# Merge, out-projection and query weights as slots of 512 columns by four channel blocks, in a two-layer hybrid backbone

## The chip, the cores and the metric

One Trainium2 chip, one core. The metric is the device time of one execution in microseconds (us), of which three were measured for the kernel before; their median counts.

## The reference, cut to what matters

Two layers run over 256 context tokens and 512 latent tokens, all of width 1024 and in float32. The weights that the change touches are those of the end of each layer's mixer, and of the query projection of the expert layer behind it:

```python
def merge(ys, gates_pre, w_branch, w_out):
    gates = jnp.split(gates_pre, N_BRANCH, axis=-1)
    acc = jax.nn.sigmoid(gates[0]) * (ys[0] @ w_branch[0])
    for i in range(1, N_BRANCH):
        acc = acc + jax.nn.sigmoid(gates[i]) * (ys[i] @ w_branch[i])
    return acc @ w_out
```

`gates_pre` are 4096 columns of the input projection `h @ w_in` (1024 by 10000), each `w_branch[i]` is 512 by 1024, `w_out` 1024 by 1024, and the query projection `peer_wq` 1024 by 2048. Behind it each token picks 128 of 16384 experts, whose rows of 1024 floats are gathered from `peer_u` (a dot product with the token) and `peer_v` (a weighted sum).

## The kernel before, in words

**Passes and tails.** Four passes run in turn: c0 and l0 (context and latent tokens of layer 0), then c1 and l1. Each ends in tails, one for each 256 tokens: c0 has one, l0 and l1 have two, c1 none. A tail is `merge` (all 16 pairs of a 256-column group j and a branch i), `outp` (out-projection, residual, second norm, transposes) and `query` (the query projection and the key scores). `merge` is written in `merge_part`, on the tensor, vector and scalar engines alike.

**Gathers beside it.** The expert layer (`peer`) is a second thread in the same programs. GpSimd issues one gather (128 rows of 4 KB) for each of the 128 slots of a token block (L3090), VectorE makes the dot product of it (L2252), TensorE sums the v rows (L1312). `side_by_side` puts so many steps of it between the pieces of a tail, by cost. Beside the second tail of l0 (stage t0) and of l1 (t1) run the 128 u gathers of the next block and their dots; beside the first tail of l0 runs the end of the expert layer of c0, with v sums on TensorE. c0's tail has the loading of later modulation weights beside it, and l1's first tail nothing: no gathers run then.

**Weight slots.** All weights go through a ring of `RING = 4` slots of 1 MB (`WRr`), in the order of `PLAN`, issued by SyncE (L3120) each as soon as the slot four places before it is marked `used`. A slot holds 256 columns by all 8 blocks of 128 input channels, so each partition gets 8 runs of 1 KB; a branch's weights (4 blocks) fill half a slot. `merge_part` on TensorE takes a gate slot and a branch slot together at the start of a unit and frees both at its end:

```python
wg = weight(("gate", pn, f, j, i_))
wb = weight(("branch", pn, f, j, i_), BB)
...
if m == 1:
    used(("gate", pn, f, j, i_))
    used(("branch", pn, f, j, i_))
```

**Results.** Each result of 128 channels by 256 tokens takes half of a PSUM bank. A gate bank is read by ScalarE (L2810, tanh into `GS`, three buffers of 256), a branch bank by VectorE (L2017 or L2020, the sum by L2022), an out-projection bank by L2048 and L2051, a query bank by L2858 or L2173. `bank` hands the banks out in turn: five where the expert layer runs beside (`BANKS`), else all eight; it waits until the last user of the bank has been read.

**Woven attention.** In c0 and in l1's first tail the merge of branches 0 to 2 is woven between the steps of the windowed attention (`attn_mix`), which in l1 takes seven banks per step from the same ring. In l0's first tail it is woven with the convolution (`conv_late`).

## Time and profile before

| what | value |
|---|---|
| runs (us) | 6261.03, 6256.57, 6257.69 |
| median | 6257.69 us |
| span of the profiled execution | 6280.9 us |
| TensorE busy | 4128.8 us (66%) |
| VectorE busy | 3226.1 us (51%) |
| GpSimd busy | 2794.8 us (44%) |
| ScalarE busy | 711.8 us (11%) |
| DMA moved | 1739.24 MB, mean 277 GB/s |
| gathers' queue q0 | 380032 packets, 1384.49 MB, 59.9% of 16 engines' span |
| SyncE's queue q1 | 314896 packets, 304.03 MB, 15.4% |

The page gives the profiled execution by its span from the first to the last instruction, and no other time of it; that span is 23.2 us (0.4%) above the median of the timed runs. Shares are averages over stages with different limits. By their instructions the five tails lie at about 364 to 685 us (c0), 1565 to 1983 (l0, first), 1983 to 2330 (l0, second, stage t0), 4197 to 4587 (l1, first) and 4587 to 4930 (l1, second, stage t1).

### The profile page before, as it was taken

Reading aid. Unit: us, or ns where it says so; the run is one execution under the profiler, and the core shown is the slowest. Engines: PE = TensorE matmul, PEld = TensorE weight load, DVE = VectorE, ACT = ScalarE, POOL = GpSimd, SP = SyncE. Lnnn points to the kernel's source line nnn. Section 1 sums busy time; section 2 is a strip of 40 time slices with the busy share of each in tenths; the row PEclk is TensorE's granted clock in tenths of the full one; section 3 lists DMA queues with packets and bytes.
Section 4 is the critical chain, followed back from the end, with each engine's and each line's share of the span. In section 5 each row is a group of like instructions: output and inputs, shape, how many; then the busy total and the mean of one; then the engine's idle time right before and its main releaser. Section 6 shows DMA issues by size and latency. Waiting matters only on the chain.

```text
span 6280.9 us, 65214 instructions
## 1 busy us (share of the span) xinstructions
PE 4128.8 (66%) x23760; PEld 2525.3 (40%) x23760; DVE 3226.1 (51%) x7726; ACT 711.8 (11%) x1572; POOL 2794.8 (44%) x2606
## 2 busy tenths in 40 slices
PE   5899767777988864544443668888977533333346
PEld 4677544335666652221110235557766300000012
DVE  3422788565625856556444216443277564654430
ACT  1221112123010011000000001233100000000000
POOL 0000243555322446767767630000034677777765
PEclk8999887889998986665555789999988755555557
DMA  6645565988886999999999971112579999999998
GB/s 221 219 156 166 190 208 199 316 312 291 290 302 231 323 340 343 355 352 360 361 367 361 368 262 43 57 43 80 171 257 326 348 353 361 369 358 365 359 367 328
DMA packets 721231, 1739.24 MB, mean 277 GB/s; under 512 B 88912, under 2 KB 371408, under 8 KB 719248
## 3 DMA queue, kind: packets, MB, share of 16 engines
q0 software_dynamic: 380032, 1384.49, 59.9%
q1 hardware_dynamic: 314896, 304.03, 15.4%
q10 hardware_dynamic: 25984, 46.56, 2.1%
q8 instruction: 189, 3.10, 0.2%
q14 instruction: 130, 1.06, 0.0%
HBM read 1706.98 MB, written 27.89 MB: 276 GB/s over the span
## 4 chain that ended last, share of the span: by engine, by line
PE 31%; issue 21%; DMA 10%; POOL 10%; DVE 9%; another core or an unknown queue 2%; ACT 2%; SPq 0%; POOLq 0%; ACTq 0%; DVEq 0%
POOL arena L3090 10%; PE bank L1219 7%; PE bank L1312 6%; DMA arena<-in_peer_v,arena 5%; PE bank L794 4%; PE bank L1273 3%; PE bank L1225 3%; DMA arena<-in_peer_u,arena 3%; DVE arena L2252 2%; PE bank L805 1%; PE bank L876 1%; PE bank L1174 1%; DMA arena<-in_w_in 1%; PE bank L1253 1%
## 5 line engine op out<-in xcount | busy, mean ns | idle before, releaser
L3090 POOL DMA_INDIRECT arena<-in_peer_u,arena x1280 | 1413.4, 1104 | 2173.6 <-DVE arena L2162 951.5
L1312 PE MATMUL bank<-arena 128*32 128x256 f32 x10240 | 1216.4, 541 | 1451.7 <-DMA arena<-in_peer_v,arena 1175.5
L2252 DVE CUSTOM_DVE_ANT_0 arena<-arena 128x1024 f32<-128x1024 f32 x1280 | 1540.5, 1223 | 1013.7 <-DMA arena<-in_peer_u,arena 922.4
L3090 POOL DMA_INDIRECT arena<-in_peer_v,arena x1280 | 1354.6, 1058 | 880.6 <-PE bank L1312 357.6
L1312 PEld LDWEIGHTS bank<-arena 128*32 128x32 f32 x10240 | 311.2, 130 | 2306.7 <-DMA arena<-in_peer_v,arena 1705.3
L1219 PE MATMUL bank<-arena 128*128 128x256 f32 x2560 | 618.3, 397 | 90.7 <-issue 55.8
L794 PE MATMUL bank<-arena 128*128 128x512 f32 (+1 forms) x1600 | 636.9, 552 | 30.2 <-issue 26.6
L1219 PEld LDWEIGHTS bank<-arena 128*128 128x128 f32 x2560 | 504.8, 200 | 187.1 <-issue 108.7
L794 PEld LDWEIGHTS bank<-arena 128*128 128x128 f32 x1600 | 320.4, 207 | 299.5 <-issue 279.4
L1225 PE MATMUL bank<-arena 128*128 128x256 f32 x1280 | 306.5, 382 | 2.3 <-ACT arena L2810 2.3
L1273 PE MATMUL bank<-arena 128*128 128x256 f32 x1280 | 292.6, 390 | 23.2 <-issue 23.2
L1273 PEld LDWEIGHTS bank<-arena 128*128 128x128 f32 x1280 | 248.2, 196 | 65.6 <-issue 31.0
L1225 PEld LDWEIGHTS bank<-arena 128*128 128x128 f32 x1280 | 239.1, 190 | 47.4 <-ACT arena L2810 13.2
L764 PE MATMUL bank<-arena 128*128 128x128 f32 x408 | 91.9, 351 | 243.9 <-DVE arena L1477 139.4
L2020 DVE SCALAR_TENSOR_TENSOR arena<-arena,bank 128x256 f32<-128x256 f32 x120 | 50.3, 420 | 340.4 <-PE bank L1225 294.3
L2893 ACT ACTIVATE arena<-arena 128x16 f32<-128x16 f32 x80 | 17.2, 216 | 1784.6 <-DVE arena L2252 1085.1
L1562 DVE SCALAR_TENSOR_TENSOR arena<-arena 128x512 f32<-128x512 f32 (+1 forms) x360 | 213.8, 658 | 5.8 <-DVE arena L1562 0.4
L805 PE MATMUL bank<-arena 128*128 128x256 f32 (+1 forms) x960 | 213.5, 382 | 2.7 <-ACT arena L2596 2.2
L805 PEld LDWEIGHTS bank<-arena 128*128 128x128 f32 x960 | 179.5, 205 | 40.1 <-issue 17.6
L764 PEld LDWEIGHTS bank<-arena 128*128 128x128 f32 x408 | 62.0, 179 | 286.3 <-issue 175.9
L1253 PE MATMUL bank<-arena 128*128 128x256 f32 x640 | 148.9, 395 | 25.7 <-issue 19.4
L3052 POOL DMA_DIRECT2D arena<-in_mod_w x20 | 15.1, 756 | 321.0 <-PE bank L832 321.0
(271 smaller groups left out, 3905.3 us busy)
## 6 DMA issues: line engine op xcount, KB each, us to landing
arena<-in_w_in SPq DMA_DIRECT2D x152, 1024.0 KB
arena<-in_mod_w POOLq DMA_DIRECT2D x20, 2048.0 KB, 11.6
arena<-in_peer_wq SPq DMA_DIRECT2D x40, 1024.0 KB
arena<-in_w_branch SPq DMA_DIRECT2D x60, 512.0 KB
arena<-in_w_out SPq DMA_DIRECT2D x20, 1024.0 KB
arena<-in_peer_u,arena POOLq DMA_INDIRECT x1280
arena<-in_peer_v,arena POOLq DMA_INDIRECT x1280
arena<-in_w_branch SPq DMA_DIRECT2D x40, 256.0 KB
```

What stands on the lines that cost most here:

```text
L764: return nc.tensor.transpose(dst, src, eye)
L794: i = mm(b[:, 0:p.n], w[:, k, m * P:(m + 1) * P], HTk(p)[:, k, :], start=(k == 0), stop=(k == KD - 1))
L805: i = mm(b[:, 0:n], HTk(p)[:, k, t * P:(t + 1) * P], w[:, k, c0:c0 + n], start=(k == 0), stop=(k == KD - 1))
L876: i = mm(b[:, 0:hi - lo], w[:, k, m * P:(m + 1) * P], HTk(p)[:, k, lo:hi], start=(k == 0), stop=(k == KD - 1))
L1219: i = mm(b[:, 0:W], wg[:, k, m * P:(m + 1) * P], HTk(p)[:, k, half], start=(k == 0), stop=(k == KD - 1))
L1225: i = mm(b[:, 0:W], wb[:, k, m * P:(m + 1) * P], YS(p, i_)[:, k, half], start=(k == 0), stop=(k == BB - 1))
L1253: i = mm(b[:, 0:W], ACC[:, k, x % 2 * P:(x % 2 + 1) * P], w[:, k, :], start=(k == 0), stop=(k == KD - 1))
L1273: i = mm(b[:, 0:W], w[:, k, m * P:(m + 1) * P], H2T[:, k, :], start=(k == 0), stop=(k == KD - 1))
L1312: i = mm(banks[6 + g // 2][32 * j:32 * j + 32, (g % 2) * W:(g % 2 + 1) * W], G["ws"][:, g, 32 * m:32 * m + 32], G["row"][ROW_BUFFER["v", i ...
L1562: v.scalar_tensor_tensor(y[:, m, :], cp[:, m, j:j + p.n], tap, y[:, m, :], ALU.mult, ALU.add)\
L2252: v.tensor_tensor_reduce(u, u, G["h2"][it % 2], 1.0, 0.0, ALU.mult, ALU.add, G["dots"][:, n:n + 1]).then_inc(*pr.step("dot", it, n))
L3090: fl.done(eng.indirect_dma_start(G["row"][x], None, table, bass.IndirectOffsetOnAxis(ids[:, n:n + 1], 0)), f"row_landed{x}", (kind + "_lan ...
```

## The change

For the tails' weights a slot becomes 512 columns by four channel blocks: runs of 2 KB, the same 1 MB, and a branch's weights now fill a slot. Gate, out-projection and query groups take two slots each (`e` = 0, 1), whose partial sums meet in the same bank; each slot is awaited where it is first used and freed after its own use. The 16 merge units of a tail become 8 units of three slots, with the same matmuls in another order. Two results of 256 share a bank, so ScalarE and VectorE read 512 columns at a time (two `GS` buffers of 512 in place of three of 256). The out-projection's matmuls have 512 moving columns in place of 256, so there are half as many. Costs that place the side thread are 3.6 for each of the six pieces of a unit. In woven tails attention and merge no longer share a ring: attention has five banks in l1 (four in c0), the merge three, the modulation one (`BESIDE`), and c0's main ring has seven.

```diff
+WIDE = 2 * W
+QK = KD // 2
...
+BESIDE = {"attn": (0, 1, 2, 5, 7), "attn_c": (0, 1, 2, 5), "merge": (3, 4, 6), "mod": (7,)}
...
-    every = [(j, i) for j in range(D // W) for i in range(4)]
+    every = [(j, i) for j in range(D // WIDE) for i in range(4)]
...
-        GS, PRD = H2[:, 0, 0:3 * W].rearrange("p (b t) -> p b t", b=3), H2[:, 0, 3 * W:4 * W]
+        GS = rows4(H2[:, 0, :], 2)
...
+        def wide(src):
+            return [(lambda w: w.rearrange("p (k n) -> p k n", k=QK), src)]
+        def plan_wide(name, a, c0):
+            for e in range(2):
+                plan(name + (e,), wide(w_view(a, KD)[:, e * QK:(e + 1) * QK, c0:c0 + WIDE]))
+        def plan_gate(l, pn, f, j, i):
+            plan_wide(("gate", pn, f, j, i), w_in[l], C_GATE + i * D + j * WIDE)
+        def plan_branch(l, pn, f, j, i):
+            plan(("branch", pn, f, j, i), branch_rows(l, i, j))
...
-                for j in range(D // W):
-                    plan(("out", pn, f, j), whole(w_view(ins["w_out"][l], KD)[:, :, j * W:(j + 1) * W]))
-                for j in range(HEADS * 256 // W):
-                    plan(("wq", pn, f, j), whole(w_view(ins["peer_wq"][l], KD)[:, :, j * W:(j + 1) * W]))
+                        plan_gate(l, pn, f, j, i)
+                        plan_branch(l, pn, f, j, i)
+                for j in range(D // WIDE):
+                    plan_wide(("out", pn, f, j), ins["w_out"][l], j * WIDE)
+                for g in range(HEADS // 2):
+                    plan_wide(("wq", pn, f, g), ins["peer_wq"][l], g * WIDE)
...
-            def bank(name):
-
-                x = taken["next"] % taken["banks"]
-                taken["next"] = x + 1
+            def bank(name, ring=None):
+                if ring is None:
+                    x = taken["next"] % taken["banks"]
+                    taken["next"] = x + 1
+                else:
+                    x = BESIDE[ring][taken[ring] % len(BESIDE[ring])]
+                    taken[ring] += 1
...
-                    ba = [bank(("as", pn, t, f, g)) for g in range(AKV)]
-                    bc = bank(("asc", pn, t, f)) if len(kb) > 4 else None
+                    ba = [bank(("as", pn, t, f, g), ring) for g in range(AKV)]
+                    bc = bank(("asc", pn, t, f), ring) if len(kb) > 4 else None
...
+                ring = "merge" if woven(p) and f == 0 and part[0][1] == 0 else None
                 for j, i_ in part:
-                    wg = weight(("gate", pn, f, j, i_))
-                    wb = weight(("branch", pn, f, j, i_), BB)
-                    for m in range(2):
-                        b = bank(("gate", pn, f, j, i_, m))
-                        for k in range(KD):
-                            i = mm(b[:, 0:W], wg[:, k, m * P:(m + 1) * P], HTk(p)[:, k, half], start=(k == 0),
-                                   stop=(k == KD - 1))
-                        i.then_inc(*mn.step("full", ("gate", pn, f, j, i_, m)))
-                        yield 3.4
-                        b = bank(("branch", pn, f, j, i_, m))
-                        for k in range(BB):
-                            i = mm(b[:, 0:W], wb[:, k, m * P:(m + 1) * P], YS(p, i_)[:, k, half], start=(k == 0),
-                                   stop=(k == BB - 1))
-                        i.then_inc(*mn.step("full", ("branch", pn, f, j, i_, m)))
-                        if m == 1:
-                            used(("gate", pn, f, j, i_))
-                            used(("branch", pn, f, j, i_))
-                        yield 1.8
+                    b = {}
+                    for e in range(2):
+                        name = ("gate", pn, f, j, i_, e)
+                        w = weight_wide(name)
+                        for q in range(2):
+                            if e == 0:
+                                b[q] = bank(("gate", pn, f, j, i_, "pair", q), ring)
+                            for m in range(2):
+                                for k in range(QK):
+                                    i = mm(b[q][:, m * W:(m + 1) * W], w[:, k, (2 * q + m) * P:(2 * q + m + 1) * P],
+                                           HTk(p)[:, e * QK + k, half], start=(e == m == k == 0), stop=(e == m == 1 and k == QK - 1))
+                            if e:
+                                i.then_inc(*mn.step("full", ("gate", pn, f, j, i_, "pair", q)))
+                            elif q:
+                                i.then_inc(*mn.step())
+                            if q:
+                                used(name)
+                            yield 3.6
+                    name = ("branch", pn, f, j, i_)
+                    w = weight_wide(name)
+                    for q in range(2):
+                        b = bank(("branch", pn, f, j, i_, q), ring)
+                        for m in range(2):
+                            for k in range(BB):
+                                i = mm(b[:, m * W:(m + 1) * W], w[:, k, (2 * q + m) * P:(2 * q + m + 1) * P], YS(p, i_)[:, k, half],
+                                       start=(k == 0), stop=(k == BB - 1))
+                        i.then_inc(*mn.step("full", ("branch", pn, f, j, i_, q)))
+                        if q:
+                            used(name)
+                        yield 3.6
...
-                    for j in range(D // W):
-                        w = weight(("out", pn, f, j))
+                    for j in range(D // WIDE):
                         b = bank(("out", pn, j, t))
-                        for k in range(KD):
-                            i = mm(b[:, 0:W], ACC[:, k, x % 2 * P:(x % 2 + 1) * P], w[:, k, :], start=(k == 0), stop=(k == KD - 1))
-                        i.then_inc(*mn.step("full", ("out", pn, j, t)))
-                        if x % 2:
-                            used(("out", pn, f, j))
-                        yield 3.5
+                        for e in range(2):
+                            w = weight_wide(("out", pn, f, j, e))
+                            for k in range(QK):
+                                i = mm(b[:, :], ACC[:, e * QK + k, x % 2 * P:(x % 2 + 1) * P], w[:, k, :],
+                                       start=(e == 0 and k == 0), stop=(e == 1 and k == QK - 1))
+                            if e:
+                                i.then_inc(*mn.step("full", ("out", pn, j, t)))
+                            elif x % 2:
+                                i.then_inc(*mn.step())
+                            if x % 2:
+                                used(("out", pn, f, j, e))
+                            yield 3.5
...
+                    if what == "quad":
+                        g, (e, q) = n[0], divmod(n[1], 2)
+                        name = ("wq", pn, f, g, e)
+                        w = weight_wide(name)
+                        if e == 0:
+                            open_[q] = bank(("wq", pn, f, "pair", 2 * g + q))
+                        for m in range(2):
+                            for k in range(QK):
+                                i = mm(open_[q][:, m * W:(m + 1) * W], w[:, k, (2 * q + m) * P:(2 * q + m + 1) * P],
+                                       H2T[:, e * QK + k, :], start=(e == m == k == 0), stop=(e == m == 1 and k == QK - 1))
+                        if e:
+                            i.then_inc(*mn.step("full", ("wq", pn, f, "pair", 2 * g + q)))
+                        elif q:
+                            i.then_inc(*mn.step())
+                        if q:
+                            used(name)
...
+            share_banks(len(banks) - 1)
...
+                    for _ in range(4):
                         yield 0
...
+                    for q in range(2):
+                        eng.wait_ge(*at("gsig", pn, f, j, i_, q))
+                        eng.wait_ge(*at("full", ("branch", pn, f, j, i_, q)))
+                        b = bank_of(("branch", pn, f, j, i_, q))
+                        acc, g = query_pair(2 * j + q), GS[:, q, :]
                         if i_ == first_branch(p, f):
...
+                            v.scalar_tensor_tensor(acc, g, 1.0, b[:, :], ALU.add, ALU.mult).then_inc(*mn.step("read", ("branch", pn, f, j, i_, q)))
                         else:
+                            v.scalar_tensor_tensor(g, g, 1.0, b[:, :], ALU.add, ALU.mult).then_inc(*mn.step("read", ("branch", pn, f, j, i_, q)))
                             eng.wait_ge(*mn.latest())
...
+                            v.tensor_tensor(acc, acc, g, ALU.add).then_inc(*mn.step())
+                        fl.mark(("gs_free", pn, f, j, i_, q), mn.sem)
...
+                past = None
                 for j, i_ in part:
...
+                    yield 0
+                    yield 0
+                    for q in range(2):
+                        if past is not None:
+                            eng.wait_ge(*at("gs_free", pn, f, *past, q))
+                        eng.wait_ge(*at("full", ("gate", pn, f, j, i_, "pair", q)))
+                        b = bank_of(("gate", pn, f, j, i_, "pair", q))
+                        act(GS[:, q, :], b[:, :], ACT.Tanh, scale=0.5).then_inc(*mn.step("gsig", pn, f, j, i_, q))
+                        fl.mark(("read", ("gate", pn, f, j, i_, "pair", q)), mn.sem)
                         yield 0
...
+                    past = (j, i_)
```

TensorE in the merge of stage t0. Names: L1219 is the gate matmul, L1225 the branch matmul before; `weights_loaded0` to `3` are the landings of the four slots, `l0_scalar` and `l0_vector` reads by the other engines. Before, one unit of 1.5 MB (256 columns of one branch):

```order
L1219 MATMUL bank2<-arena 128x256 [waits l0_scalar,weights_loaded3,weights_loaded2]
L1219 MATMUL bank2<-arena 128x256 x7
L1225 MATMUL bank3<-arena 128x256 [waits l0_scalar]
L1225 MATMUL bank3<-arena 128x256 x3
L1219 MATMUL bank4<-arena 128x256 [waits l0_vector]
L1219 MATMUL bank4<-arena 128x256 x7
L1225 MATMUL bank0<-arena 128x256 [waits l0_scalar]
L1225 MATMUL bank0<-arena 128x256 x3
```

and now one unit of 3 MB (512 columns), with L1255 for gates and L1270 for branches:

```order
L1255 MATMUL bank2<-arena 128x256 [waits l0_scalar,weights_loaded3]
L1255 MATMUL bank2<-arena 128x256 x7
L1255 MATMUL bank3<-arena 128x256 [waits l0_scalar]
L1255 MATMUL bank3<-arena 128x256 x7
L1255 MATMUL bank2<-arena 128x256 [waits weights_loaded0]
L1255 MATMUL bank2<-arena 128x256 x7
L1255 MATMUL bank3<-arena 128x256 x8
L1270 MATMUL bank4<-arena 128x256 [waits l0_scalar,weights_loaded1]
L1270 MATMUL bank4<-arena 128x256 x7
L1270 MATMUL bank0<-arena 128x256 [waits l0_vector]
L1270 MATMUL bank0<-arena 128x256 x7
```

Before, one instruction waits for two slots every 24 matmuls; now each slot is awaited alone, with 16 matmuls on each, and between the last matmul into a bank and the first of its next use lie 32 to 48 other matmuls in place of 24.

TensorE in the first tail of l1, where an attention step (from L1140) follows a merge piece. Before:

```order
L1219 MATMUL bank4<-arena 128x256 [waits l1_vector,weights_loaded1,weights_loaded0]
L1219 MATMUL bank4<-arena 128x256 x7
L1140 MATMUL bank7<-arena 128x128 [waits l1_scalar,l1_vector]
L1144 MATMUL bank5<-arena 128x256
L1144 MATMUL bank6<-arena 128x256
L1146 MATMUL bank5<-arena 128x128
L1146 MATMUL bank6<-arena 128x128
L1150 MATMUL bank5<-arena 128x128
L1150 MATMUL bank6<-arena 128x128
L1155 MATMUL bank7<-arena 128x128 [waits l1_tensor]
```

and now (the step begins at L1171):

```order
L1255 MATMUL bank6<-arena 128x256 [waits weights_loaded1]
L1255 MATMUL bank6<-arena 128x256 x7
L1255 MATMUL bank3<-arena 128x256 x8
L1171 MATMUL bank0<-arena 128x128 [waits l1_scalar,l1_vector]
L1175 MATMUL bank5<-arena 128x256
L1175 MATMUL bank7<-arena 128x256
L1177 MATMUL bank5<-arena 128x128
L1177 MATMUL bank7<-arena 128x128
L1181 MATMUL bank5<-arena 128x128
L1181 MATMUL bank7<-arena 128x128
L1186 MATMUL bank0<-arena 128x128 [waits l1_tensor]
```

The bank of the first score (`asc`), taken by the step's first instruction, is now `bank0`, which the copy of the first transposed probabilities of the previous step (ScalarE L2755 before) has to have read; before it was the bank of eight allocations ago.

## Rows read from the trace of the kernel before

**Rows 1.** The page, 40 slices of 157 us: DMA in tenths, rate.

```profile
DMA  6645565988886999999999971112579999999998
GB/s 221 219 156 166 190 208 199 316 312 291 290 302 231 323 340 343 355 352 360 361 367 361 368 262 43 57 43 80 171 257 326 348 353 361 369 358 365 359 367 328
```

**Rows 2.** Busy us of each engine by stretch, clock, DMA share, rate.

```profile
1565.00:1827.00 262.00, 261.33 (x1537) 170.52 (x1537) 122.88 (x201) 23.47 (x48) 91.08 (x91) 1.00 0.88 290
...
2011.00:2207.00 196.00, 159.54 (x669) 134.75 (x667) 159.95 (x428) 12.68 (x33) 98.93 (x82) 0.90 0.96 335
2207.00:2262.00 55.00, 33.61 (x145) 28.88 (x145) 40.82 (x76) 5.29 (x10) 21.24 (x18) 0.81 0.93 329
2262.00:2330.00 68.00, 64.17 (x321) 56.93 (x321) 42.71 (x81) 12.37 (x22) 31.84 (x27) 0.98 0.99 360
2011.00:2330.00 319.00, 257.32 (x1134) 220.55 (x1132) 243.48 (x584) 30.33 (x65) 152.01 (x126) 0.90 0.96 339
...
4612.00:4930.00 318.00, 257.10 (x1134) 220.39 (x1133) 240.78 (x578) 30.60 (x65) 152.05 (x127) 0.90 0.95 331
```

**Rows 3.** Waits of 2011 to 2207 us: total, times, longest.

```profile
PE bank L1219 <- issue: 28.3, 8, 7.8
...
DVE arena L2252 <- DMA arena<-in_peer_u,arena: 10.2, 3, 8.1
...
PE bank L1219 <- DMA arena<-in_w_branch: 7.5, 1, 7.5
```

**Rows 4.** Timeline, SyncE queue and TensorE, 2071 to 2092 us: start, us.

```profile
2071.22 0.37 SPq L3120 DMA_DIRECT2D arena<-in_w_in  x1
2071.64 2.29 SPq L3120 DMA_DIRECT2D arena<-in_w_branch  x2
2083.63 0.37 SPq L3120 DMA_DIRECT2D arena<-in_w_in  x1
...
2091.43 2.04 PE L1219 MATMUL bank<-arena 128*128 128x256 f32 x4 [7.84 <-issue]
```

**Rows 5.** DMA queues, 2011 to 2330 us: packets, MB, share of 16 engines.

```profile
q0 software_dynamic: 18432, 67.12, 57.2%
q1 hardware_dynamic: 36068, 36.95, 35.5%
```

**Rows 6.** The same, 4612 to 4930 us.

```profile
q1 hardware_dynamic: 33216, 34.08, 33.1%
```

**Rows 7.** The same, 4197 to 4466 us, with no gathers.

```profile
q1 hardware_dynamic: 24096, 24.12, 29.8%
```

**Rows 8.** The same, 5000 to 6200 us, gathers almost alone.

```profile
q0 software_dynamic: 117423, 427.54, 95.0%
```

**Rows 9.** Chain that ended last, 1820 to 1985 us: start, us.

```profile
1838.04 16.56 DMA arena<-in_norm_g
```

**Rows 10.** Timeline, 1845 to 1880 us, first out-projection of l0.

```profile
1856.66 6.40 PE L1253 MATMUL bank<-arena 128*128 128x256 f32 x16 [6.30 <-DVE arena L2048]
...
1877.73 0.86 PEld L764 LDWEIGHTS bank<-arena 128*128 128x128 f32 x8 [4.13 <-DVE arena L2062]
```

**Rows 11.** Groups of instructions by line: busy, mean ns, idle before.

```profile
L1219 PE MATMUL bank<-arena 128*128 128x256 f32 x2560 | 618.3, 397 | 90.7 <-issue 55.8 <-DMA arena<-in_w_branch 16.6 <-DVE arena L2111 7.1
...
L2810 ACT ACTIVATE arena<-bank 128x256 f32<-128x256 f32 x160 | 61.1, 382 | 773.1 <-PE bank L1219 698.4 <-issue 25.2 <-DVE arena L2158 22.9
...
L2020 DVE SCALAR_TENSOR_TENSOR arena<-arena,bank 128x256 f32<-128x256 f32 x120 | 50.3, 420 | 340.4 <-PE bank L1225 294.3 <-issue 26.7 <-ACT arena L2760 15.9
...
L2755 ACT ACTIVATE arena<-bank 128x512 f32<-128x512 f32 x64 | 34.8, 589 | 4.6 <-PE bank L1174 3.3 <-remote 1.3
...
L1422 DVE TENSOR_TENSOR arena<-bank,arena 128x512 f32<-128x512 f32 x26 | 18.0, 691 | 0.9
```

**Rows 12.** Waits of 4197 to 4466 us, second layer, first half.

```profile
PE bank L1174 <- ACT arena L2772: 21.3, 16, 2.3
...
PE bank L1225 <- ACT arena L2810: 2.3, 5, 0.5
```

134 lines of the change are left out of this document (57 added, 77 removed).

## The prediction

> **What bounds the kernel now.** I read the page's slices first: between about 2000 and 3600 us, and again from about 4600 us to the end, the DMA row stands at 8 or 9 tenths and the rate near 340 to 370 GB/s [rows 1]. Those are the stretches with expert gathers. The tails that the change touches lie partly inside them, so I asked for busy times by stretch next. In stage t0 (second tail of l0) the DMA share is 0.96 from the first gather at 2011 us to the end at 2330 us, while TensorE is busy 257.3 of 319 us and VectorE 243.5. In t1 it is 0.95 of 318 us, TensorE 257.1 [rows 2]. So both stages are bound by the DMA engines, not by an engine that computes. In l0's first tail it is the other way: TensorE is busy 261.3 of 262 us in the merge, at DMA share 0.88 [rows 2].
>
> The waits say how TensorE feels the full DMA. In the merge of t0 it lost 28.3 us "issue" in 8 waits and 7.5 us to a branch weight [rows 3]; "issue" is idle time for which the profile shows no releaser, and the timeline tells what it is: SyncE issued a gate and a branch slot at 2071.22 and 2071.64, the unit before ended when the next two slots were issued, at 2083.63, and TensorE went on only at 2091.43 [rows 4]. These waits are late weights. VectorE on the other side waited only 10.2 us for u rows [rows 3]: the gathers are ahead, the weights behind.
>
> **The change, part by part.** All against a span of 6280.9 us, which is 23.2 us above the median of the runs; the terms are taken off the median, since 0.4% of any of them is nothing.
>
> *Runs of 2 KB.* The bytes stay, the number of runs halves. Price of a run of 1 KB inside t0: q1 took 35.5% of 319 us, 113 us, for 36.95 MB, so 16 x 113 us / 36.95 MB, 50 ns per run. A gather row of 4 KB there took 57.2% of 319 us x 16 / 67.12 MB, 178 ns [rows 5]. A straight line through both has a fixed part of 7.5 ns per run, so runs of 2 KB save 3.7 of 50 ns, 7.5%, which is 8.4 us of t0. The other end comes from stretches where each queue is nearly alone: 54.5 ns per KB without gathers (24.12 MB in 29.8% of 269 us) and 175 ns per row of the gathers (427.54 MB in 95.0% of 1200 us) [rows 7, 8]. That gives a fixed part of 14.4 ns and a saving of 13%, 15 us. I take 11 us, between them, since the two pairs of rows are about equally near; in t1, with q1 at 33.1% of 318 us [rows 6], 10 us. As the stages are bound by this, the saving is on the path: 21 us, with ends 16 and 28.
>
> The Trainium skill ("DMA: Bandwidth & Descriptors", Why small descriptors are slow) gives each packet about 3 cycles on top of one per 32 bytes: 35 for 1 KB against 67 for 2 KB, an estimate of 4% or 9 us for both stages, by which the time would be 12 us higher than my forecast. No row here counts cycles.
>
> *Slots freed one by one, all four full.* Now at most two slots are asked for when a unit ends; after the change each slot has three others' work, 48 matmuls, to land in, against 24. It fills the idle DMA time, at most 4% of 319 us (13 us) in t0 and 5% of 318 us (16 us) in t1 [rows 2]. Some of it stays: barriers between stages (t0's out-projection has TensorE busy for 33.6 of 55 us, at DMA share 0.93 [rows 2]), and the time in which VectorE's dots hold the gathers. I take a third, 9 us for both; ends 0 and 29.
>
> *Out-projection.* Half as many matmuls, twice as wide: the same columns, so TensorE's time stays. In l0's first tail the chain waits 16.56 us for the row of the second norm [rows 9], and VectorE reads no out-projection bank before it, so TensorE runs out of its five banks and stands 6.30 us [rows 10]. Now four results need four banks, so it does not stand; and one slot rather than two is ahead of the norm rows in the queue when the merge ends. 1 MB costs 3.3 us alone (24.12 MB in 80 us [rows 7]) and 8.6 us beside gathers (36.95 MB in 319 us [rows 5]). What comes behind, a wait of 4.13 us of the last transposes for VectorE [rows 10], is late next. I take 4 us; ends 0 and 9. c0 and l1 have no gathers beside their out-projection and gain nothing.
>
> *Reads of 512.* An instruction of 256 columns takes 382 ns on ScalarE and 420 ns on VectorE, one of 512 takes 589 and 691 ns [rows 11]: less in all, but VectorE is not the bound. At a stage's end the last result waits for two of 691 in place of two of 420 ns, 0.54 us more. At three such ends each in c0 and l1's first tail nothing covers that: 3.3 us lost. The gates' longer hold and the two `GS` buffers cost nothing, since ScalarE waits for TensorE there (698.4 us of waits before L2810 [rows 11]); were that cover gone, it would be 0.2 us a read.
>
> *Bank rings in the woven tails.* In l1 the first instruction of an attention step now waits for ScalarE's copy of the first transposed probabilities. Where a gate has just ended (every third step, 5 of them) ScalarE does a tanh of 512 and then that copy, 589 ns each [rows 11]: 1.2 us x 5, 6 us lost. Against that, 2.3 us of waits of branch matmuls for gate reads go [rows 12]. Ends: 0 and 12 us. In c0 a step takes four banks from a ring of four, read a whole step before, so nothing. The modulation's own bank is read at once after its group; nothing.
>
> Sum: -21 - 9 - 4 + 3 + 4 = -27 us, and 6257.7 - 27 = 6231 us.
>
> **Rivals.** *A, the weights catch up altogether.* Here two queues share an engine run by run. 1 KB of weights against a row of 4 KB then has 50 of 228 ns, 16 x 1024 B in 228 ns or 72 GB/s, and the late fetch of [rows 4], 1.57 MB in some 18 us (87 GB/s), is near it. With 2 KB it would be 93 of 271 ns, 121 GB/s: 25.2 MB of merge weights come in 208 us, and most idle DMA time goes. All high ends: -28 - 29 - 9 + 3 = -63, 6195 us. Against it: VectorE must find its dots' rows in what is left. The Trainium skill ("DMA: Bandwidth & Descriptors", Queues, rings and completion order) says that an engine drains a whole packet of some 9 to 17 descriptors before it turns to another queue, by which the length of a run need not change the share as the line through [rows 5] has it; no row here shows the turns.
>
> *B, the wait moves.* What the weights gain the gathers lose: VectorE, which hardly waits for rows now [rows 3], waits for them, the branch banks are read later, and only the cheaper runs at their low end remain, without the 4 us. -16 + 7 = -9, 6249 us. For it speaks the share of 0.96 [rows 2]: there is little left to hand over.
>
> *C, slower: the small rings.* If each attention step of l1 (16) and c0 (8) waits for ScalarE's or VectorE's read, as TensorE already does once per step (21.3 us in 16 waits, the longest 2.3 [rows 12]), by 2.3 us, that is 55 us against the 34 gained: 6279 us. It decides from 34 / 24 = 1.4 us a step. Against it: the order shows only every third step with a gate's tanh in the way.
>
> *D, the runs are not 2 KB.* Should the queue cut them to 1 KB again, the 21 us go: 6252 us.
>
> **How the numbers follow.** Forecast 0.50, A 0.20, B 0.17, C 0.10, D 0.03. The likeliest case gives 6231 us and by itself reaches from about 6215 to 6245. The range goes down to A and up to just short of C: 6194 to 6266 us. A measurement of this kernel can tell about 0.2%, 12.5 us, from no change. Faster by more: nearly all of the forecast, and A: 0.68. Within: B, D and the forecast's upper edge: 0.21. Slower: C and a little: 0.11.
>
> **What would show it.** Right: q1's packets fall by about 90,000 (five tails of 36,864 runs of 1 KB, halved) at the same MB; t0 and t1 are each some 15 us shorter at an unchanged DMA share near 0.96; the "issue" waits of the gate line there shrink below 15 us; the stand of 6.30 us is gone; l1's first tail is some 5 us longer. Wrong: t0 and t1 unchanged with VectorE's waits for u rows grown (B), or shorter by 28 us and more (A); attention steps in l1 and c0 with a wait before each first score (C); q1 with as many packets as before (D).

## The result, and the profile after

The changed kernel takes 6214.5 us (median of 4 runs, 6209.27 to 6220.0); the kernel before, run beside it, takes 6258.6 us (6256.57 to 6261.03). The ratio is 0.9929, with a 95% interval from 0.9915 to 0.9943: 44 us faster. The forecast was 6231 us with 6194 to 6266 as its range; what was measured lies about half way between it and rival A's 6195 us.

The page of the kernel after, span 6212.5 us (the execution itself 6214.72 us); the second line shown is DMA in tenths over 40 slices:

```profile
PE 4094.5 (66%) x23440; PEld 2448.4 (39%) x23440; DVE 3201.4 (52%) x7526; ACT 693.6 (11%) x1470; POOL 2814.9 (45%) x2606
...
DMA  6555465898996989999999971122479999999999
...
q0 software_dynamic: 380032, 1384.49, 60.3%
q1 hardware_dynamic: 221936, 304.03, 15.0%
```

q1 carries the same 304.03 MB in 92,960 fewer packets, as announced, so rival D is out. Its share of the whole span hardly moved, and no share on the page tells where 44 us went. For that I measured each tail from TensorE's timeline, from its first gate matmul to the start of what follows it: the next layer or tail for the first tails, the first v sum for t0 and t1. c0's tail is taken to the start of its last query matmul:

| us | before | before, run again | after | after, run again |
|---|---|---|---|---|
| c0, tail | 305.2 | 305.4 | 306.2 | 308.1 |
| l0, first tail | 418.4 | 418.5 | 409.3 | 411.8 |
| l0, second tail (t0) | 389.5 | 388.9 | 371.2 | 371.6 |
| of it, merge to the first out-projection matmul | 231.3 | 230.2 | 212.0 | 212.4 |
| l1, first tail | 390.8 | 391.0 | 391.5 | 391.5 |
| l1, second tail (t1) | 358.6 | 351.9 | 338.8 | 336.6 |

The three tails beside gathers give 9 or 7, 17 to 18 and 13 to 22 us, together 43 on the mean. For t1 the spread is wide because the two executions of the kernel before differ by 6.7 us there. The rest of the program, mostly gathers alone, scatters by 10 us and more from one execution to the next (the last 1330 us took 1334.7 and 1325.6 before, 1317.9 and 1324.8 after), so I leave it out. In t0 the whole gain lies before the out-projection. Busy times there (columns as in [rows 2]: busy us of TensorE, its weight loads, VectorE, ScalarE and GpSimd, then clock, DMA share and GB/s; the second row is TensorE's idle piece at the merge's end):

```profile
2000.00:2152.00 152.00, 143.28 (x651) 123.66 (x649) 133.95 (x362) 9.36 (x18) 81.38 (x71) 0.99 1.03 381
2152.00:2184.00 32.00, 0.19 (x1) 0.22 (x2) 31.59 (x53) 0.60 (x1) 17.98 (x12) 0.53 0.96 344
2184.00:2232.00 48.00, 32.55 (x80) 15.20 (x80) 32.13 (x56) 5.28 (x10) 20.78 (x17) 0.82 0.80 290
2232.00:2301.00 69.00, 64.49 (x321) 57.17 (x321) 42.85 (x78) 11.68 (x18) 32.64 (x26) 0.97 0.97 349
2000.00:2301.00 301.00, 240.51 (x1052) 196.25 (x1050) 240.52 (x547) 26.92 (x47) 152.78 (x126) 0.91 0.97 355
```

In these first 152 us the DMA engines move 381 GB/s; in the 152 us from 2011 us of the kernel before they moved 333, and in its whole merge 335 [rows 2]. Then TensorE stands for 32 us in which VectorE is busy for 31.59. The waits in the merge of t0, of TensorE and of VectorE, to be held against [rows 3]:

```profile
PE bank L1298 <- DVE arena L2077: 32.0, 1, 32.0
PE bank L1255 <- DVE arena L2169: 4.9, 1, 4.9
...
PE bank L1270 <- DMA arena<-in_w_branch: 1.3, 1, 1.3
```

```profile
DVE arena L2310 <- DMA arena<-in_peer_u,arena: 13.0, 7, 8.1
```

Each line gives the total, how many waits, and the longest. The late weights are gone: 28.3 us of "issue" and 7.5 us for a branch weight have become 1.3 us. In their place stands one wait of 32.0 us: the first out-projection matmul (L1298) needs the last sum of the merge (L2077). The timelines of TensorE and of VectorE there:

```profile
2139.74 3.62 PE L1255 MATMUL bank<-arena 128*128 128x256 f32 x16
2144.68 7.17 PE L1270 MATMUL bank<-arena 128*128 128x256 f32 x32 [1.33 <-DMA arena<-in_w_branch]
2183.81 2.90 PE L1298 MATMUL bank<-arena 128*128 128x512 f32 x3 [31.95 <-DVE arena L2077]
```

```profile
2154.71 1.22 DVE L2310 CUSTOM_DVE_ANT_0 arena<-arena 128x1024 f32<-128x1024 f32 x1
...
2156.37 2.29 DVE L2188 TENSOR_TENSOR arena<-arena 128x2048 f32<-128x2048 f32 x1
2158.70 2.77 DVE L2194 TENSOR_TENSOR arena<-arena 128x256 f32<-128x256 f32 x8
2161.50 2.29 DVE L2196 TENSOR_REDUCE arena<-arena 128x128 f32<-128x2048 f32 x1
...
2182.30 0.69 DVE L2075 SCALAR_TENSOR_TENSOR arena<-arena,bank 128x512 f32<-128x512 f32 x1
2183.02 0.69 DVE L2077 TENSOR_TENSOR arena<-arena 128x512 f32<-128x512 f32 x1
```

TensorE has its last branch result ready near 2152 us. VectorE reads it at 2182.30, behind dots (L2310) and routing work (L2188 to L2196) that its order puts ahead, and it is never idle meanwhile. In t1 it is the same: TensorE's idle piece is 27.5 us, and VectorE is busy for 27.6 of the 28 us from 4736 us. So in the kernel after, VectorE ends the merges of t0 and t1.

What did it wait for before? The kernel before, VectorE in the merge of t0 (1983.3 to 2214.6 us):

```profile
DVE arena L2020 <- issue: 19.1, 4, 8.0
```

L2020 reads a branch result. Each of the four waits ended 0.1 us after TensorE's last matmul into that result (L1225), and each such result followed a wait of TensorE that [rows 3] counts as "issue": for those 19.1 us VectorE stood for results that TensorE could not yet make. They are as long as the whole difference: 231.3 - 19.1 = 212.2, against 212.0 us measured. That fit is in part luck, since two smaller changes cancel: VectorE's busy time fell from 191.4 to 188.7 us, and its waits for gathered rows grew from 10.2 to 13.0. The second execution of the kernel before, with a merge of 230.2 us, has 19.5 us of the same waits:

```profile
DVE arena L2020 <- issue: 11.1, 4, 4.8
...
DVE arena L2017 <- PE bank L1225: 8.4, 2, 4.4
```

That is the theory the experiments are to test: **late weights cost this stage only through VectorE's idle time; the DMA engines do not bound it.** Its rival is the sentence of the prediction, "both stages are bound by the DMA engines".

### The profile page after: what moved, and what is told of

The parts are those of the page before. It is cut to its first block and busy times, and to the rows that moved or that the text cites. A ratio compares the mean times of both kernels' runs of the same rounds, so it can differ in the third digit from the quotient of the medians.

```text
span 6212.5 us, 63979 instructions
## 1 busy us (share of the span) xinstructions
PE 4094.5 (66%) x23440; PEld 2448.4 (39%) x23440; DVE 3201.4 (52%) x7526; ACT 693.6 (11%) x1470; POOL 2814.9 (45%) x2606
## 3 DMA queue, kind: packets, MB, share of 16 engines
q1 hardware_dynamic: 221936, 304.03, 15.0%
q14 instruction: 126, 1.03, 0.0%
## 5 line engine op out<-in xcount | busy, mean ns | idle before, releaser
L1369 PE MATMUL bank<-arena 128*32 128x256 f32 x10240 | 1203.4, 538 | 1433.9 <-DMA arena<-in_peer_v,arena 1181.6
L2310 DVE CUSTOM_DVE_ANT_0 arena<-arena 128x1024 f32<-128x1024 f32 x1280 | 1540.5, 1223 | 1035.7 <-DMA arena<-in_peer_u,arena 911.2
L1255 PE MATMUL bank<-arena 128*128 128x256 f32 x2560 | 579.0, 385 | 25.1 <-DVE arena L2169 12.3
L1255 PEld LDWEIGHTS bank<-arena 128*128 128x128 f32 x2560 | 487.7, 193 | 109.5 <-issue 42.0
L1326 PE MATMUL bank<-arena 128*128 128x256 f32 x1280 | 293.5, 391 | 27.4 <-issue 27.4
L1270 PE MATMUL bank<-arena 128*128 128x256 f32 x1280 | 290.5, 384 | 8.6 <-DVE arena L2073 3.6
L1270 PEld LDWEIGHTS bank<-arena 128*128 128x128 f32 x1280 | 243.1, 192 | 50.4 <-issue 5.0
L785 PE MATMUL bank<-arena 128*128 128x128 f32 x408 | 93.0, 354 | 229.9 <-DVE arena L1534 129.5
L1298 PE MATMUL bank<-arena 128*128 128x512 f32 x320 | 145.2, 612 | 63.8 <-DVE arena L2077 32.0
L2075 DVE SCALAR_TENSOR_TENSOR arena<-arena,bank 128x512 f32<-128x512 f32 x60 | 41.2, 686 | 274.9 <-PE bank L1270 273.9
L785 PEld LDWEIGHTS bank<-arena 128*128 128x128 f32 x408 | 63.1, 181 | 271.8 <-issue 171.4
```

The lines of the kernel that those rows point to most:

```text
L785: return nc.tensor.transpose(dst, src, eye)
L1255: i = mm(b[q][:, m * W:(m + 1) * W], w[:, k, (2 * q + m) * P:(2 * q + m + 1) * P], HTk(p)[:, e * QK + k, half], start=(e == m == k == 0), ...
L1270: i = mm(b[:, m * W:(m + 1) * W], w[:, k, (2 * q + m) * P:(2 * q + m + 1) * P], YS(p, i_)[:, k, half], start=(k == 0), stop=(k == BB - 1))
L1298: i = mm(b[:, :], ACC[:, e * QK + k, x % 2 * P:(x % 2 + 1) * P], w[:, k, :], start=(e == 0 and k == 0), stop=(e == 1 and k == QK - 1))
L1326: i = mm(open_[q][:, m * W:(m + 1) * W], w[:, k, (2 * q + m) * P:(2 * q + m + 1) * P], H2T[:, e * QK + k, :], start=(e == m == k == 0), st ...
L1369: i = mm(banks[6 + g // 2][32 * j:32 * j + 32, (g % 2) * W:(g % 2 + 1) * W], G["ws"][:, g, 32 * m:32 * m + 32], G["row"][ROW_BUFFER["v", i ...
```

## The experiments

They ran in three groups, each beside the kernel before: 6253.5 us for e0 to e3, 6048.4 us for e4 to e7, 6262.2 us for e8 to e11. Why the second group is 3.3% shorter is taken up at the end; within a group the ratio counts, across groups the length of the tails, which did not change with it.

**e0, the kernel before again.**

> The kernel before, once more, with a profile: a control. Both theories: no difference from the runs of before. Its profile is to show how far the stretches of two executions of one program differ: the first profile of before was 22 us longer than the median of its runs, and the stretch of pure gathers at the end (L1312 from 4946 us on) was 17 us longer there than in the changed kernel. If that is scatter, this profile has that stretch within 5 us of the changed kernel's 1318 us.

It took 6251.9 us, ratio 0.9989 (0.9976 to 1.0003). This is what no change looks like. Its tails stand in the table above. Its stretch of pure gathers at the end took 1325.6 us, not within 5 us of the changed kernel's 1318 as expected, but 9 us shorter than in the first execution of the same program: scatter, and more of it than expected.

**e1, runs of 1 KB again.** Each slot of 512 columns comes as two transfers of 256 columns (four for the attention branch); slots, order and freeing stay as changed, in all five tails.

```diff
...
-            return [(lambda w: w.rearrange("p (k n) -> p k n", k=QK), src)]
+            return [((lambda w, h=h: w.rearrange("p (k n) -> p k n", k=QK)[:, :, h * W:(h + 1) * W]),
+                     src[:, :, h * W:(h + 1) * W]) for h in range(2)]
```

> The changed kernel with each wide slot loaded by two DMAs of 256 columns (four for the attention branch), so that the runs are 1 KB again; slots, banks and order stay. Theory 1 (cheaper runs carry most of the gain): 21 us slower than the changed kernel, 6235 us, with the DMA share of t0 unchanged and its length up by 10 us. Theory 2 (slots freed one by one, all four full, carry it): within 6 us of 6214.5 us. Theory 3 (share of an engine by run: with 1 KB the weights get 50 of 228 ns beside gathers): over 30 us slower, and the waits of the gate line for weights are back.

It took 6213.3 us, ratio 0.9928 (0.9912 to 0.9943), not to be told from the changed kernel's 0.9929: theory 2's forecast, and far from the other two. t0 took 371.0 us, merge to out-projection 211.9. The same stretch as the last row above, TensorE's waits and VectorE's in the merge, and q1 in the stretch:

```profile
2000.00:2301.00 301.00, 247.62 (x1049) 199.10 (x1047) 240.25 (x547) 27.14 (x47) 151.37 (x125) 0.93 1.00 355
```

```profile
PE bank L1257 <- DMA arena<-in_w_in: 11.5, 6, 5.3
PE bank L1272 <- DMA arena<-in_w_branch: 10.7, 5, 5.0
```

```profile
DVE arena L2077 <- PE bank L1272: 4.6, 2, 3.8
```

```profile
q1 hardware_dynamic: 35477, 36.00, 36.8%
```

The runs of 1 KB cost what they were said to cost: q1 took 0.368 x 301 / 36.00 = 3.08 us of all 16 engines per MB, against 0.327 x 301 / 35.56 = 2.77 us with runs of 2 KB (19696 packets of q1 in that stretch, 35.56 MB, 32.7%), 11% more. The weights were later by 21 us as well. Neither reached the end of t0, because TensorE had 32 us to spare. In t1, where it had 27.5, a little did: the merge to the out-projection took 210.8 us against 207.8 and 207.5 in the two executions of the changed kernel, with 7.0 us of VectorE's waits for late results, where the changed kernel has none:

```profile
DVE arena L2077 <- PE bank L1272: 7.0, 2, 5.2
```

From the changed kernel to e1 the DMA share of the stretch rose from 0.97 to 1.00 at the same 355 GB/s: a high share did not mean that the engines had nothing left to give.

**e2, slots freed together.** In the second tails the two gate slots are marked used only with the branch slot, at the unit's end.

```diff
-                            if q:
+                            if q and f == 0:
                                 used(name)
...
                         if q:
+                            if f:
+                                for e in range(2):
+                                    used(("gate", pn, f, j, i_, e))
                             used(name)
```

> The changed kernel, but in the second tails of l0 and l1 (t0 and t1) the three slots of a merge unit are freed together at its end, as before. Theory 1: the depth gave 9 us, so 6223 us, waits of the gate line for weights come back to some 15 us per tail. Theory 2: 30 us slower, 6245 us. Theory 3: under 5 us slower, since weights of 2 KB runs arrive fast enough.

It took 6206.7 us, ratio 0.9922 (0.9908 to 0.9936), the changed kernel's again; here theory 3's forecast came out, so no theory has both e1 and e2. t0 took 371.1 us, though TensorE waited:

```profile
PE bank L1255 <- DMA arena<-in_w_in: 15.9, 7, 3.7
PE bank L1301 <- issue: 10.3, 1, 10.3
PE bank L1270 <- DMA arena<-in_w_branch: 6.5, 4, 2.3
```

In t1 the merge to the out-projection took 211.1 us, 3 more than in the changed kernel, as in e1, and VectorE waited there:

```profile
DVE arena L2078 <- PE bank L1270: 5.3, 2, 3.9
```

**e3, both undone.**

> Both edits together. Theory 1: the two add up, 30 us slower than the changed kernel, 6245 us, so most of the 44 us is gone; what is left comes from out-projection and reads. Theory 2: as much slower as with the freeing alone. Theory 3: as much slower as with the short runs alone.

It took 6234.2 us, ratio 0.9966 (0.9954 to 0.9978): 21 us more than e1 and 28 more than e2. t0 took 383.6 us and t1 352.3. TensorE's waits in the merge of t0, then VectorE's:

```profile
PE bank L1257 <- DMA arena<-in_w_in: 17.8, 7, 4.4
PE bank L1272 <- DMA arena<-in_w_branch: 12.8, 2, 7.5
PE bank L1303 <- issue: 9.8, 1, 9.8
```

```profile
DVE arena L2080 <- PE bank L1272: 7.6, 3, 3.2
DVE arena L2080 <- issue: 4.3, 1, 4.3
DVE arena L2078 <- PE bank L1272: 3.6, 2, 3.2
```

With both undone VectorE stands 15.5 us for late results, and merge to out-projection is 223.9 us, 11.9 over the 212.0 of the changed kernel. With one undone it stood 4.6 us (e1) or not at all (e2) and there was no loss. In t1 each alone cost 3 us, and both together 13 (221.0 us, with 16.5 us of such waits). So the two remedies are not terms of a sum, and none of the three theories foretold that: either alone brings nearly all weights inside VectorE's time, and the second has little or nothing left to give.

**e4, narrow out-projection results.** Weights stay in wide slots; each result of 256 columns has its own bank, and VectorE reads 256 columns at a time.

```diff
-                        b = bank(("out", pn, j, t))
+                        b = [bank(("out", pn, j, h, t)) for h in range(2)]
...
-                                i = mm(b[:, :], ACC[:, e * QK + k, x % 2 * P:(x % 2 + 1) * P], w[:, k, :],
+                                    i = mm(b[h][:, 0:W], ACC[:, e * QK + k, x % 2 * P:(x % 2 + 1) * P],
+                                           w[:, k, h * W:(h + 1) * W],
...
```

> The changed kernel with the out-projection's results 256 columns wide again, one bank for each and VectorE reading 256 at a time; the weights stay in wide slots. Theory (the out-projection gained because TensorE hands over and VectorE reads half as many, twice as large results): the out stage of l0's first tail goes from 33.8 us back to about 43, the other out stages by 0 to 3, the kernel by +8 to +14 us, to about 6226. Rival (it gained because its weights, and the merge's ring of banks ahead of it, are no longer late): the out stage stays within 3 us and the kernel within 5 us of the changed one, 6209 to 6220.

It took 6006.2 us, ratio 0.9933 (0.9917 to 0.9949), not to be told from the changed kernel's 0.9929. So the rival's forecast came out and the theory's 8 to 14 us did not. l0's first tail took 412.2 us, hardly more than the changed kernel's 409.3 and 411.8 and far from the 418.5 of before; from its first out-projection matmul to its first query matmul it took 51.4 us, against 50.9 and 50.6 in the changed kernel and 59.5 and 59.0 before; the matmuls themselves span 37.5 us, against 34.4 and 44.0. But the row of the second norm landed earlier in this execution, which can hide a loss. VectorE's first work behind that row, in the changed kernel and in e4:

```profile
1848.32 1.23 DVE L2096 SCALAR_TENSOR_TENSOR arena<-arena 128x1024 f32<-128x1024 f32 x1 [23.05 <-DMA arena<-in_norm_g]
...
1868.16 0.69 DVE L2091 COPY arena<-bank 128x512 f32<-128x512 f32 x1 [0.91 <-PE bank L785]
```

```profile
1814.07 1.22 DVE L2100 SCALAR_TENSOR_TENSOR arena<-arena 128x1024 f32<-128x1024 f32 x1 [18.95 <-DMA arena<-in_norm_g]
...
1840.56 0.69 DVE L2095 COPY arena<-bank 128x512 f32<-128x512 f32 x1 [1.53 <-PE bank L785]
```

From the row to the last copy it is 20.5 us with wide results, 27.2 with narrow ones, 24.8 in the kernel before (1854.72 to 1879.56). VectorE's wait for the row was 26.91 us before, 23.05 after, 18.95 here. So of the 8.6 us from 59.5 to 50.9, 3.9 are the earlier row and 4.3 the shorter way from it to the last copy. The earlier row is not scatter: it landed 26.8 and 26.9 us after the first out-projection matmul in the two executions of before, and 22.6 to 22.9 in nine of the twelve with the change in them (18.9 to 21.4 in the other three, 18.9 being e4's). That the 4.3 us come from wide results is argued from the rows behind the norm, not shown by the time of e4.

**e5, dots spread.** The cost of a merge piece in the second tails is 2.8 in place of 3.6, so `side_by_side` puts less of the side thread between them: 70 dots in place of 78 in the merge of t0, and three blocks of routing work (L2188 to L2196) in place of four.

```diff
-                            yield 3.6
+                            yield 3.6 if f == 0 else 2.8
...
-                        yield 3.6
+                        yield 3.6 if f == 0 else 2.8
```

> The changed kernel with the cost of a unit of the second tails' merges set from 3.6 to 2.8, which moves some 8 of the 83 units of routing and dots out of each merge into the out-projection and the query (a dot keeps VectorE for 1.30 us, 1220 ns and 82 ns). Theory (the merge of t0 and t1 ends at VectorE since the weights are in time): merge and gap together fall from 212 us by about 10, out and query absorb the dots in VectorE's idle time (43 of 117 us there), so t0 and t1 are each 8 to 10 us shorter and the kernel takes about 6195 to 6199 us. Rival (the DMA engines bound the whole stage, share 0.97 between 2000 and 2301): what the merge gains, out and query give back; the kernel within 5 us of the changed one.

It took 5983.1 us, ratio 0.9896 (0.9878 to 0.9915): the lowest ratio of all kernels that compute the reference. t0 took 364.0 us and t1 331.7, each 7 us less than in the changed kernel (7.6 and 4.9 less than in its second execution), where the theory had 8 to 10. The merge of t0, and TensorE's wait at its end:

```profile
1946.70:2140.50 193.80, 172.81 (x770) 147.72 (x770) 171.54 (x422) 12.64 (x23) 92.16 (x77) 0.95 0.96 350
```

```profile
PE bank L1298 <- DVE arena L2077: 14.1, 1, 14.1
```

VectorE is busy 17.2 us less in the merge (188.7 before this edit), the merge is 18.2 us shorter, and 11.0 us of it come back behind. The dots now lie ahead of the norm, whose wait by TensorE (L785) grew to 19.0 us. No transfer was made smaller or dropped, only the order of VectorE's work was changed, with the gathers that follow it: that order bounds the merge.

**e6, more for VectorE.** One more instruction of 512 columns, without effect, behind each result of the second tails' merges.

```diff
+                        if f == 1:
+                            eng.wait_ge(*mn.latest())
+                            v.tensor_tensor(acc, acc, acc, ALU.max).then_inc(*mn.step())
```

> The changed kernel with one more VectorE instruction of 512 columns, of no effect, behind each result of the second tails' merges: 16 of 691 ns in each, 11.1 us. Theory (VectorE bounds these merges): t0 and t1 are each 9 to 11 us longer, the kernel takes 6233 to 6237 us. Rival (the DMA engines bound them; VectorE waits 13 us for gathered rows in the merge, and would spend the new work there): each at most 3 us longer, the kernel within 6 us of the changed one.

It took 6017.0 us, ratio 0.9945 (0.9928 to 0.9961). t0 took 380.1 us and t1 346.1, 8.9 and 7.3 us more than after, just under the 9 to 11 of the theory and far over the rival's 3. The new line in the merge of t0, and TensorE's wait:

```profile
L2080 DVE TENSOR_TENSOR arena<-arena 128x512 f32<-128x512 f32 x16 | 11.1, 691 | 0.5
```

```profile
PE bank L1298 <- DVE arena L2080: 34.0, 1, 34.0
```

Of 11.1 us of new work 8.6 show in the merge (220.6 us in place of 212.0). The rest went into VectorE's waits for gathered rows, 10.0 us in place of 13.0. The wait grew by 2 us only, since TensorE's matmuls were held up too (7.2 us for L2075 in place of 4.8).

**e7, half of each gate slot loaded.** In the second tails only two of the four channel blocks of each gate slot are loaded; the rest of the slot keeps what it held.

```diff
...
+            for e in range(2):
+                plan(("gate", pn, f, j, i, e), [((lambda w: w.rearrange("p (k n) -> p k n", k=QK)[:, 0:2]),
+                                                 w_view(w_in[l], KD)[:, e * QK:e * QK + 2, c0:c0 + WIDE])])
```

> The changed kernel with only half of each gate slot loaded in the second tails' merges (2 of 4 pieces of 128 input channels; the rest of the slot keeps what it held, so the gates of these halves are computed from wrong weights). 16 slots of 1.05 MB halved are 8.4 MB less in each of t0 and t1, at the 355 GB/s of 2000 to 2301 some 24 us of the DMA engines. Theory (VectorE bounds the merge once the weights are in time): merge and gap stay near 212 us, less what VectorE waited for gathered rows (13 us); the kernel is 0 to 15 us faster, 6200 to 6215. Rival (both stages are bound by the DMA engines): t0 and t1 each about 20 us shorter, the kernel near 6175.

It took 5989.4 us, ratio 0.9904 (0.9886 to 0.9922). 16.8 MB fewer were loaded; t0 took 364.3 us and t1 334.9, 7 and 4 us less, where a DMA-bound stage would have lost 20 to 24 each. So the bytes are not free, but they are worth between a sixth and a third of that. TensorE still stood 32.0 us for L2077's counterpart. VectorE's wait for gathered rows fell from 13.0 to 7.9 us, which is 5.1 of the 6.1 us by which the merge got shorter.

**e9, the changed kernel again, and e8, fewer bytes with the dots spread.** e8 joins the edits of e5 and e7, so it too leaves out half of each gate slot.

> The changed kernel itself, as the measure for the three beside it. Ratio to the kernel before as at first, 0.993; t0 371 us, t1 338 us.

> Cost 2.8 for the second tails' merge units (dots spread, as in e5_dots_spread) and only half of each of their gate slots loaded (as in e7_gate_half_loaded; the gates of the other halves are computed from wrong weights). Theory (the DMA engines are not what ends t0 and t1, even with the dots spread): the fewer bytes give what they gave alone, 4 to 7 us in each; t0 about 358 us, t1 about 327 us. Rival (once VectorE is relieved, the DMA engines at share 0.96 to 0.98 bound the stage): the bytes now give 12 to 24 us in each, t0 340 to 352 us.

e9 took 6211.5 us, ratio 0.9920 (0.9903 to 0.9937). e8 took 6192.8 us, ratio 0.9894 (0.9875 to 0.9912), with t0 at 358.4 and t1 at 329.2 us: 5.6 and 2.5 us less than e5, as the theory had it. Bytes are worth no more with VectorE relieved than without, and it is again its wait for rows that fell, 12.4 to 7.5 us.

**e10, more dots spread** (cost 2.4), **and e11, dots moved into the query** (2.2 for the merge, 1.5 and 1.0 for the out-projection).

> Cost 2.4 instead of 2.8, some 5 more dots of 1.30 us out of each second merge. Theory (what is left of TensorE's stand at the end of the merge, 14.1 us, is VectorE's): merge and gap fall from 193.8 to about 187 us; out-projection and query, where VectorE is now busy 80 of 113 us, give back 3 to 6 us; t0 and t1 within 3 us of 364 and 331.7 us. Rival (the moved dots find free time in VectorE there): t0 and t1 each 6 us shorter again.

> Costs for the second tails of 2.2 (merge), 1.5 and 1.0 (out-projection and its transposes), 3.6 (query) as it was: about 73 units of dots in the merge, 10 beside the out-projection and 49 in the query, where cost 2.8 gave 75, 18 and 39. Theory (VectorE's order sets each part's end): the wait for the norm's rows before the query falls from 26 us to below 20, the query stage (VectorE busy 37 of 57 us) takes the ten dots at nearly no cost: t0 355 to 360 us. Rival (the query is bound by the DMA engines at share 0.98, and dots need 4 KB rows): what the out-projection gains is lost in the query and behind it; t0 364 to 370 us.

e10 took 6205.8 us, ratio 0.9910 (0.9890 to 0.9931); e11 6198.8 us, ratio 0.9908 (0.9890 to 0.9926). Their merges of t0:

```profile
1973.60:2158.20 184.60, 173.32 (x769) 148.50 (x769) 157.32 (x397) 12.74 (x23) 84.59 (x72) 0.96 0.96 347
```

```profile
1973.30:2155.80 182.50, 173.17 (x770) 148.03 (x771) 161.44 (x405) 12.86 (x23) 87.11 (x75) 0.98 0.95 346
```

The merges reach 184.6 and 182.5 us, near TensorE's own 173. But e10's wait for the norm (L785) grew to 24.1 us, and t0 is back at 367.5 us and t1 at 336.3, 3.5 and 4.6 more than e5. In e11 that wait fell to 5.5 us, the weights of the out-projection were late instead (8.4 us), and from the last query matmul to the next v sums 69.6 us passed where e5 had 57.1. t0 took 366.1 us, as e11's rival had it. For t1 neither side gave a number; there the way behind the query grew by 4 us only, and the tail took 325.8 us, 5.9 less than in e5. e5 ran in another group than e8, e10 and e11, and all their intervals overlap. That e5 beats the changed kernel is shown by its tails. The intervals alone do not settle it: 0.9878 to 0.9915 lies below the 0.9915 to 0.9943 of the changed kernel's first group, but overlaps e9's 0.9903 to 0.9937. That e5 beats e11 is not shown either: e5 has the lower ratio, but t0 and t1 together are 691.9 us in e11 and 695.7 in e5.

## Why the prediction was right, and the step that was wrong

The time lay in the range and the forecast's side was right, 16.5 us short of the gain and just outside the 6215 to 6245 that the likeliest case was given. That the sum came so close is partly luck. Its terms were 30 us for t0 and t1, 4 for l0's first tail and 7 lost elsewhere; the tails moved by 35, 8 and 2 on the mean. And its largest term rests on a step that is wrong. By its own steps:

*Runs of 2 KB.* The size was right, the place was not. It took 11 us of DMA time in t0 for the saving; 3.08 - 2.77 us per MB is 0.31, for 36 MB 11 us. The step that failed is the one after it: "As the stages are bound by this, the saving is on the path". e1 gives the saving back, and neither its time (6213.3 us) nor t0 shows a loss, only t1 one of 3 us. What ended these merges was VectorE, and the gain was its idle time behind late results, 19.1 us in t0. The step rested on a DMA share of 0.96; the changed kernel reaches 1.03 at 381 GB/s over 152 us, so 0.96 was no ceiling. The Trainium skill's fixed cost per packet ("DMA: Bandwidth & Descriptors", Why small descriptors are slow), which gave an estimate of 4%, is too small here: the saving measured is 10% of the 3.08 us per MB.

*Slots freed one by one.* The waits it aimed at did vanish (35.8 to 1.3 us), but e2 shows that the freeing alone is worth nothing in t0 and 3 us in t1 while the runs are long. By e3 the two together are worth 12 us in t0 and 14 in t1. The prediction's sums, 11 + 4.5 and 10 + 4.5, came near that by chance: taken away alone, each term is worth 0 to 3 us.

*The gathers are ahead, the weights behind.* This reading of [rows 3] held, and with it rival B fell: VectorE's wait for rows went from 10.2 to 13.0 us only, and its 6249 us did not come. Rival A, the weights catching up altogether, described the weights rightly (1.3 us of waits left), but its price did not follow: it put t0 and t1 at 57 us less together, and they gave 33 to 38, as the wait moved on to VectorE. Its mechanism, two queues that share an engine run by run, is the third theory of e1, which had over 30 us lost by 1 KB runs; that did not come. The prediction took VectorE for unbound, since it was busy 243.5 of 319 us in the stage [rows 2]; but in the merge it was busy 191.4 of 231.3 us, and 29.3 us of the rest were its waits for late results and for rows.

*Out-projection.* Forecast 4 us, measured 8.6 in l0's first tail: 3.9 from the earlier norm row and 4.3 behind it, of which e4 leaves open how much the wide results give. The stand of 6.30 us for a bank is gone, and in e4, with narrow results, one of 3.0 us is back. That c0 and l1 gain nothing here was wrong: from the first out-projection matmul to the first query matmul c0 went from 41.0 to 38.6 us and l1's first tail from 40.5 to 38.1.

*Reads of 512 and bank rings.* Forecast 7 us lost in all (5 in l1, 2 in c0). l1's first tail is 0.5 to 0.7 us longer, and that is a sum of two signs: its merge is 2.2 us longer (270.1 to 272.3 us), the query part about 1, and the out-projection gives the 2.4 us back. c0's tail is 1 to 3 us longer, no more than its scatter (304.3 to 308.1 us over all runs with the change in it). Attention's waits in l1 are as they were, 19.1 us in 15 waits against 21.3 in 16 [rows 12]:

```profile
PE bank L1205 <- ACT arena L2830: 19.1, 15, 2.3
PE bank L1222 <- ACT arena L2813: 3.6, 4, 1.8
PE bank L1171 <- ACT arena L2813: 2.7, 2, 1.3
```

The 6 us of tanh ahead of the copies was over-sized: the new waits for those copies come to 2.7 and 3.6 us, and the whole merge lost 2.2. Rival C is out by the same rows.

What stays open is the rest between e3 and the kernel before: 5 to 6 us in t0, 0 to 6 in t1, for which the prediction had no term. They differ in the size of a unit and in VectorE's reads, and no run separates these. The reads of 512 do take VectorE less time, 188.75 us of busy time in e3's merge of t0 against 191.4 before; the prediction set that at nothing since it held VectorE not to be the bound.

## What to carry to other kernels

Before a saving is put on the path, ask which engine ends the stage if the wait is cured: sum each engine's busy time up to the stage's last result, not over the stage, and see whose order stands behind that result. Two remedies for one wait can share its price, so undo each alone and both together before crediting either. After a wait is gone, re-tune the costs that place background work; here one number (3.6 to 2.8) gave another 12 to 14 us of tails for nothing.

## What the runs showed of the hardware

- **A DMA share near 1 is no ceiling.** The merge of t0 before, with weights in 1 KB runs and gathers, moved 335 GB/s at share 0.96. Over 152 us of it the changed kernel, with 2 KB runs, moved 381 GB/s at 1.03, and e1, with 1 KB runs, 371 GB/s at 1.05. Over 301 us e1 has share 1.00 and the changed kernel 0.97 at the same 355 GB/s. The share is the summed time of the packets over that of 16 engines, so a value above 1 means that packet times overlap: it says how long packets were under way, not what was left.
- **Gathers alone ran at two speeds.** In the group of e4 to e7 the stretch of pure gathers took 1224 to 1228 us, in the others 1318 to 1335. Busy times of e9 and e5 there:

```profile
5000.00:6100.00 1100.00, 447.54 (x3258) 100.30 (x3251) 527.60 (x1070) 16.93 (x41) 808.45 (x750) 0.52 0.97 364
```

```profile
4900.00:5900.00 1000.00, 438.07 (x3265) 83.20 (x3261) 500.63 (x997) 16.72 (x40) 769.73 (x741) 0.51 1.01 392
```

  364 against 392 GB/s, under the same program there. The tails did not move with it: t0 of e4 took 371.1 us, of the changed kernel 371.2. That is one more sign that the transfers do not end them. The three groups ran on three different chips (the one of e4 to e7 is the fast one, by the kernel before too: 6048.4 us against 6253.5 and 6262.2). Whether the rate belongs to the chip, no run shows.
